# Gated linear attention with stacked gate products, transferred rotation of the queries and halved square sums, in a two-block network on one core

## The reference, cut to what matters

```python
g = log_sigmoid(lowrank @ w_gk + b_gk) / 16        # forward and backward, rank 16 each
q = apply_rope(rms_norm_2(q, q_norm), cos, sin)    # a head's quarters 0,1 and 2,3 change places
p = softmax(q @ k.T * 128 ** -0.5)
o, _ = gla_chunked(q_g, k_g, v_g, g, s0)           # forward and backward, added
y = rms_norm_2(o, g_norm) * silu(gate)             # a head is 256 wide: two tiles of 128
```

## Time and profile before

| what | us |
|---|---|
| median of 3 runs (2815.57 to 2822.95) | 2822.2 |
| the profiled execution, its own time | 2820.59 |
| its span, first to last instruction | 2818.8 |
| PE busy in the span | 2741.7 (97%) |
| DVE busy | 1572.7 (56%) |
| ACT busy | 861.2 (31%) |
| one head, from one `gate_z(·, 0)` to the next (1891.21 to 2004.09) | 112.9 |

### The profile page before, as it was taken

One profiled execution on the slowest core, in us unless ns is written; L12 is line 12 of the kernel. 1 busy time (PEld: TensorE's weight loads), 2 busy tenths in 40 slices (PEclk: granted clock), 3 DMA queues, 4 the chain that ended last, 5 costly groups with the idle time before them and its releaser, 6 DMA issues.

```text
span 2818.8 us, 33294 instructions
## 1 busy us (share of the span) xinstructions
PE 2741.7 (97%) x12970; PEld 2287.3 (81%) x12970; DVE 1572.7 (56%) x2127; ACT 861.2 (31%) x958; POOL 75.7 (3%) x151
## 2 busy tenths in 40 slices
PE   6999999999999999999999999999999999999999
PEld 5888878888888888888788887788888888778887
DVE  5745547636577366645763445667666533564433
ACT  3222234112142121422322323454545522332211
POOL 0000000000000000000000000000000000000000
PEclk9999999999999999999999999999999999999999
DMA  7634523635436355322453422111111342223222
GB/s 279 240 125 171 198 86 117 227 104 203 157 124 230 113 181 183 106 98 96 157 198 101 149 90 96 46 38 57 53 39 43 122 146 96 83 90 103 92 100 79
DMA packets 92935, 353.46 MB, mean 125 GB/s; under 512 B 10528, under 2 KB 11296, under 8 KB 84000
## 3 DMA queue, kind: packets, MB, share of 16 engines
q1 hardware_dynamic: 73120, 250.05, 26.4%
q0 software_dynamic: 19280, 101.23, 9.9%
q10 hardware_dynamic: 432, 0.75, 0.1%
HBM read 343.60 MB, written 8.39 MB: 125 GB/s over the span
## 4 chain that ended last, share of the span: by engine, by line
PE 89%; DVE 6%; ACT 2%; issue 1%; DMA 1%; SPq 0%; DVEq 0%; ACTq 0%
PE ps L1832 23%; PE ps L1834 23%; PE ps L1833 23%; PE ps L2017 4%; PE ps L2019 4%; PE ps L2018 4%; PE ps L2259 1%; DMA w_raw<-in_units 1%; DVE w_raw_lo L1040 1%; PE ps L2207 1%; DVE h_lo L1176 1%; DVE w_lo L1040 0%; PE ps L2112 0%; ACT w_hi L592 0%; PE ps L2253 0%
## 5 line engine op out<-in xcount | busy, mean ns | idle before, releaser
L1832 PE MATMUL ps<-h_hi,w_hi 128*128 128x512 f32 x1936 | 756.5, 391 | 10.8 <-DVE h_lo L1176 4.6
L1833 PE MATMUL ps<-h_lo,w_hi 128*128 128x512 f32 x1936 | 754.7, 390 | 0.0
L1834 PE MATMUL ps<-h_hi,w_lo 128*128 128x512 f32 x1936 | 754.7, 390 | 0.0
L592 ACT CAST w_hi<-w_raw 128x2048 fp32r<-128x2048 f32 (+1 forms) x240 | 422.0, 1758 | 616.4 <-PE ps L1834 520.9
L1040 DVE TENSOR_TENSOR w_lo<-w_raw,w_hi 128x2048 fp32r<-128x2048 f32 (+1 forms) x219 | 458.3, 2093 | 132.5 <-ACT w_hi L592 132.3
L1832 PEld LDWEIGHTS ps<-h_hi,w_hi 128*128 128x128 f32 x1936 | 364.4, 188 | 90.2 <-issue 11.0
L1834 PEld LDWEIGHTS ps<-h_hi,w_lo 128*128 128x128 f32 x1936 | 364.3, 188 | 76.3
L1833 PEld LDWEIGHTS ps<-h_lo,w_hi 128*128 128x128 f32 x1936 | 364.5, 188 | 75.3
L1832 PE MATMUL ps<-g_hi,w_hi 128*128 128x512 f32 x960 | 373.5, 389 | 0.0
L1833 PE MATMUL ps<-g_lo,w_hi 128*128 128x512 f32 x960 | 373.4, 389 | 0.0
L1834 PE MATMUL ps<-g_hi,w_lo 128*128 128x512 f32 x960 | 373.4, 389 | 0.0
(11 more groups left out here) (331 smaller groups left out, 2931.2 us busy)
## 6 DMA issues: line engine op xcount, KB each, us to landing
w_raw<-in_units SPq DMA_DIRECT2D x350, 512.0 KB, 4.5
ada<-in_ada_t POOLq DMA_DIRECT2D x56, 1024.0 KB, 6.9
w_raw<-in_units SPq DMA_DIRECT2D x128, 352.0 KB, 3.7
ada<-in_ada_t POOLq DMA_DIRECT2D x64, 512.0 KB, 5.0
ada_first<-in_ada_t SPq DMA_DIRECT2D x8, 1024.0 KB, 18.1
x_res<-in_x SPq DMA_DIRECT2D x4, 512.0 KB, 8.1
x_home<-x_res POOLq DMA_DIRECT2D x1, 2048.0 KB, 6.5
attn_home<-attn_out POOLq DMA_DIRECT2D x8, 256.0 KB, 2.3
```

The costliest lines, as they stand in the source:

```text
L592: nc.scalar.copy(W_HI[u.slot][:, 0:n], W_RAW[u.slot][:, 0:n]).then_inc(hi_done, 1)
L1832: pe.matmul(dst, hi[:, k, c], rhs_hi(k), start=(k == 0), stop=False)
L1833: pe.matmul(dst, hi[:, k, c], rhs_lo(k), start=False, stop=False)
L1834: last = pe.matmul(dst, lo[:, k, c], rhs_hi(k), start=False, stop=(k == kt - 1))
```

## The change

1. **Stacked gate products.** `U_LR` holds the low-rank weights three times (96 columns, unit of 768 columns instead of 256). ACT rounds its result into `LRT` (96 rows, two copies), and DVE replaces rows 32 to 63 by the rest. The gate's weights come as 96 rows, already block-diagonal, into the scratch `SSQ` by one transfer; ACT rounds them (`gate_weights_hi`), DVE forms the rest in rows 64 to 95 (`gate_weights_lo`). `gate_z` is then one fp32r product over 96 rows (hi·hi + lo·hi + hi·lo). GpSimd's clearing of `W_GK` goes. On SP the first of these loads waits for `ms_made` 7 (end of L2008) and not for `wgk_zero`.
2. **Rotation by transfers.** The two products with PERM go. SP copies `QX` to `TQ` in eight transfers of 32 partitions by 512 (`swap_queries`), behind `q_evac`; `q_turned` waits for `q_swapped` and reads `TQ` instead of the banks. `q_root` waits for the squares alone (`q_ms`).
3. **Squares added on VectorE.** `out_sums` adds the two tiles of squares; `out_squares` on PE has four products instead of eight.
4. **Five-part queries.** `queries` has parts of 1, 2, 1, 2 and 2 blocks k; the first stands ahead of `gate_z(i+1, 0)`, the others around the gate and norm products.
5. **One exp-ln set.** Before the gate's first Exp, ACT loads a set that holds Exp and Ln, so that L814 and the first `decay` Exp behind it need no load.
6. Order: ACT's `split_hi` and DVE's `split_lo` of the next head's value unit (U_G+4i+6) move ahead of `decay_in(·, 0)` and of `q_scale`. Some semaphores are merged (no change of order).

```diff
-    return KD * 2 * RANK if n == U_LR else FULL
+    return KD * GATE_ROWS if n == U_LR else FULL
...
                 if i == 0:
-                    sp.wait_ge(wgk_zero, 1)
+                    sp.wait_ge(ms_made, 7)
...
+                sp.dma_start(W_GK_RAW, ins["w_gk"][:, i, :]).then_inc(wgk_landed, 16)
+
+            def swap_queries(i):
+                sp.wait_ge(q_evac, i + 1)
+                for m in range(2):
+                    for b in range(4):
+                        sp.dma_start(TQ[m][32 * b:32 * b + 32, :], QX[m][32 * (b ^ 1):32 * (b ^ 1) + 32, :]).then_inc(q_swapped, 16)
...
+            def gate_weights_hi(i):
+                act.wait_ge(wgk_landed, 16 * (i + 1))
+                if i > 0:
+                    act.wait_ge(z_made, 2 * i)
+                nc.scalar.copy(W_GK[0:GATE_ROWS].rearrange("p d m -> p (d m)"), W_GK_RAW).then_inc(wgk_hi, 1)
...
             def gate_exp(i, d):
+                if d == 0:
+                    nc.scalar.preload_act_table_set("natural_log_exp_and_others")
...
+            def gate_weights_lo(i):
+                low = slice(4 * RANK, GATE_ROWS)
+                dve.wait_ge(wgk_hi, i + 1)
+                w = W_GK[low].rearrange("p d m -> p (d m)")
+                nc.vector.tensor_tensor(w, SSQ[low, 0:2 * P], w.bitcast(F32), ALU.subtract).then_inc(wgk_made, 1)
...
+            def out_sums(i):
+                dve.wait_ge(o_sq, 2 * i + 2)
+                nc.vector.tensor_tensor(O_SQ[0], O_SQ[0], O_SQ[1], ALU.add).then_inc(o_ssq, 1)
...
             def q_turned(i, m):
+                dve.wait_ge(q_swapped, 128 * (i + 1))
                 nc.vector.tensor_tensor(QX[m][:], QX[m][:], COS[:], ALU.mult)
-                nc.vector.tensor_tensor(TQ[m][:], BANK[4 + m], SIN[:], ALU.mult).then_inc(q_sin, 1)
+                nc.vector.tensor_tensor(TQ[m][:], TQ[m][:], SIN[:], ALU.mult).then_inc(q_sin, 1)
...
-                for m in range(2):
-                    last = pe.matmul(BANK[4 + m], PERM[:], QX[m][:], start=True, stop=True)
-                last.then_inc(q_rot, 1)
...
                 for c in range(NC_):
-                    for e in range(2):
-                        last = pe.matmul(BANK[2][:, c:c + 1], O_SQ[e][:, c * CH:(c + 1) * CH], ONES_D[:, 1:2], start=(e == 0), stop=(e == 1))
+                    last = pe.matmul(BANK[2][:, c:c + 1], O_SQ[0][:, c * CH:(c + 1) * CH], ONES_D[:, 1:2], start=True, stop=True)
...
                 if i + 1 < GH_:
+                    queries(i + 1, 0)
                     gate_z(i + 1, 0)
-                    queries(i + 1, 0)
+                    queries(i + 1, 1)
                     out_squares(i)
+                    queries(i + 1, 2)
                     gate_z(i + 1, 1)
-                    queries(i + 1, 1)
+                    queries(i + 1, 3)
                     out_scales(i)
-                    queries(i + 1, 2)
+                    queries(i + 1, 4)
                     gk_gq(i + 1, 0)
-                    query_turns(i + 1)
+                    query_squares(i + 1)
```

More of the change, by code:

```diff
@@ L406, in build @@
         q_evac = sem("q_evac")
+        o_ssq = sem("o_ssq")
+        q_swapped = sem("q_swapped")
         v_made = sem("v_made")
@@ L484, in _ @@
             ffn(3)
-            unit(at(U_LR), KD * 2 * RANK)
+            unit(at(U_LR), KD * GATE_ROWS)
             sp.wait_ge(evac_done, U_LR)
@@ L927, in rounds @@
                 out_squares(i)
+            low_rank_hi()
+            gate_weights_hi(0)
             split_hi(at(U_K))
@@ L939, in _ @@
             key_root()
-            decay(0, 0)
-            decay(0, 1)
+            decay_out(0, 0)
+            decay_in(0, 0)
+            decay_out(0, 1)
+            decay_in(0, 1)
             kq_out(0)
@@ L1707, in _ @@
                     decay_arg(i + 1, 1)
+                    split_lo(at(U_G + 4 * i + 6))
                     q_scale(i + 1)
@@ L1710, in _ @@
                     q_turned(i + 1, 1)
-                    split_lo(at(U_G + 4 * i + 6))
                     decayed(i + 1, 0)
@@ L2111, in gate_z @@
                 for a, b in ((0, T), (T, TA)):
-                    last = pe.matmul(PS[:, 6 * T + a:6 * T + b], W_GK[0:2 * RANK, d, :], LRT[0:2 * RANK, a:b], start=True, stop=True)
+                    last = pe.matmul(PS[:, 6 * T + a:6 * T + b], W_GK[0:GATE_ROWS, d, :], LRT[0:GATE_ROWS, a:b], start=True, stop=True)
                 last.then_inc(z_made, 1)
@@ L2122, in queries, with query_squares @@
                     pe.wait_ge(lo_done, u.v + 1)
-                last = h_products(u, [BANK[4], BANK[5]], (range(0, 3), range(3, 6), range(6, 8))[part])
-                if part == 2:
+                last = h_products(u, [BANK[4], BANK[5]], (range(0, 1), range(1, 3), range(3, 4), range(4, 6), range(6, 8))[part])
+                if part == 4:
                     last.then_inc(pe_done, 1)
-            def query_turns(i):
+            def query_squares(i):
                 pe.wait_ge(z_out, 2 * i + 2)
@@ L2133, in query_turns @@
                     for c in range(4):
-                        pe.matmul(BANK[6][:, 4 * m + c:4 * m + c + 1], Q_SQ[m][:, c * P:(c + 1) * P], ONES_HD[:, 0:1], start=True, stop=True)
-                pe.wait_ge(q_evac, i + 1)
-                for m in range(2):
-                    last = pe.matmul(BANK[4 + m], PERM[:], QX[m][:], start=True, stop=True)
-                last.then_inc(q_rot, 1)
+                        last = pe.matmul(BANK[6][:, 4 * m + c:4 * m + c + 1], Q_SQ[m][:, c * P:(c + 1) * P], ONES_HD[:, 0:1], start=True, stop=True)
+                last.then_inc(q_ms, 1)
             def own_scores(i):
@@ L2332, in _ @@
             own_scores(0)
-            for part in range(3):
+            for part in range(5):
                 queries(0, part)
-            query_turns(0)
+            query_squares(0)
             for i in range(GH_):
@@ L2464, in feature_tiles, with gate_rows @@
     return np.asarray(rows)[0].T.reshape(KD, P, -1).transpose(1, 0, 2)
+def gate_rows(inputs):
+    w = np.zeros((3, 2 * RANK, GH_, 2, P), np.float32)
+    for d, name in enumerate(("w_gk_fwd_2", "w_gk_bwd_2")):
+        w[:, RANK * d:RANK * (d + 1), :, d, :] = np.asarray(inputs[name])[0].reshape(RANK, GH_, P)
+    return w.reshape(GATE_ROWS, GH_, 2 * P)
 def layouts(inputs):
```

105 lines of the change are left out of this document (59 added, 46 removed).

## The result

The changed kernel takes 2795.08 us (median of 4 runs, 2794.94 to 2795.95), the kernel before beside it 2820.39 us (2815.57 to 2822.95): a ratio of 0.9912, 95% interval 0.9897 to 0.9926. The prediction was 2794.5 us. The profiled execution has a span of 2793.4 us, against 2818.8 before.

What follows compares the result with a forecast made beforehand. TensorE (PE), busy in 97% of the span, was taken as the bound. Terms 24.6 (8.2 x 3) + 3.9 + 0.8 - 0.65 - 1.2 - 1.35 = 26.1 us off 2820.59 gave 2794.5, range 2786 to 2808.

Steps and rivals of the forecast that it cites:

- two gate products: Each change of heads, TensorE: two plain float32 products become one fp32r product each, 1.33 us saved twice, 2.66.
- clock: Each change of heads: the granted clock's drop to 0.50 behind squares and second gate product goes, 1.6 us saved.
- value weights' wait: Each change of heads: TensorE's wait for the value unit's rest goes, as split_lo comes ahead of the rotation, 0.9 us.
- VectorE's margin: Changes of heads: VectorE's 3.68 us in hand before the first row maximum are used up to 0.2 us.
- The transfers: The queries' rotation: eight transfers issued one every 0.475 us, each landing 2.2 us after issue.
- Head 0: Gates save 3.9 us; the rotation loses 0.65 by a later start and 1.2 by half clock after idling.
- Ahead of head 0: U_V's issue waits for ms_made 7, loss 1.0 us; the wider low-rank unit on VectorE, 0.35; 1.35 lost in sum.
- Behind head 3: Behind the last head: ScalarE's 0.78 us wait for the squares goes, 0.8 us saved.
- Transfers landing late: Rival, chance 0.12: the last transfer takes 5.0 us instead of 2.2 to land, 10.5 us lost, so 2805.
- The clock still dropping: Rival, chance 0.10: the clock still drops at each change of heads, 3 x 1.6 us back, 2799.
- The rounds taking part back: Rival, chance 0.06: VectorE enters the rounds without its 3.68 us; with 1.5 us more per head, 2800.
- Not doing what it says, or slower: Slower, chance 0.02: the rotation becomes the bound; 10 us of landing gives 2825. Same has 0.02 too.

Runs made afterwards that it cites:

- e3: The changed kernel with the gate products of the same 96 stacked rows as plain float32 products: 2804.01 us.
- e11: e6 with the gate products over 32 rows of plain float32 values, as in the kernel before, instead of 96: 2812.6 us.
- e5: The changed kernel with the queries in the three parts of before, squares and second gate product side by side: 2797.24 us.
- e4: The changed kernel with the squares of a head's two halves summed on TensorE again, without VectorE's addition: 2797.42 us.
- e1: The changed kernel with the queries' rotation back on TensorE in every head (two PERM products behind the squares), no transfers: 2796.49 us.
- e6: The changed kernel with the edits of e1, e3, e4 and e5 together; table set, split_lo order and gate weights' path stay: 2808.32 us.
- e9: The changed kernel with the value weights' rest (split_lo) behind the rotation on VectorE again: 2818.56 us, ratio to the kernel before 0.9995.
- e8: The changed kernel with each of the eight transfers cut in two, sixteen of 16 partitions, to land about 5 us later: 2815.47 us.
- e7: The changed kernel without the combined table set of exponential and logarithm: 2799.46 us.
- e2: The changed kernel with PERM products on TensorE in head 0 alone and transfers in heads 1 to 3: 2792.21 us.
- e10: The changed kernel with head 0's gate weights issued behind the value unit U_V instead of ahead of it: 2794.44 us.
- c1: The changed kernel with PERM products in head 0 alone, as in e2, and ScalarE's v_out ahead of the fourth level's exponentials: 2784.95 us, ratio to before 0.9878.

## Why the prediction held, term by term

**A change of heads.** Predicted 8.4 on TensorE, 8.2 taken; measured 8.4 (25.3 in three).

| term | predicted | measured | from |
|---|---|---|---|
| two gate products | 2.66 | 2.4 | e3 1.9 + 0.5 of e11 for the 32 rows |
| wait for `at_made`, with the order | 0.5 | 0.7 | e5 |
| squares | 0.85 | 1.0 | e4 |
| permutation | 1.9 | 1.7 | e1 |
| clock | 1.6 | 1.6 | e11, first change against the others |
| value weights' wait | 0.9 | 1.2 | what is left: before 45.2, e11 with its drop 44.0 |
| sum | 8.4 | 8.6 | 45.19 - 36.75 = 8.4 by the marks |

The sizes hold to 0.3 us each. The gate term was a little high: from a gate product's start to the second product behind it the trace before has 1.79 and 1.82 us (the prediction gives 1.69), the trace after 0.59, so two save 2.4 and not 2.66. One reason is not shown: the clock's. That the drop would go was right, and so was its price. But parting the pieces is not needed (no drop in e5 and e6), and two of e11's three changes have the pair in full and no drop. Whether shortening it is what took the drop away stays open; that the term came out as large as predicted is in part luck. The last term is a remainder, not measured by an edit that undoes it alone; e9 does not give it, since with the transfers that order costs 8.1.

**VectorE's margin.** "Used up to 0.2, so every us by which transfers land later is lost in each head": the size holds in e8, 5.0 us in each change and its rounds for 5.2 us of delay. The mechanism is shown by e7 and not by e8: in e7 VectorE's 0.55 us turn up as 0.6 in the rounds at full clock, while in e8 the 1.8 us of the rounds are at the same time TensorE's half clock behind its wait, a term that the prediction had for head 0 alone. The layout put the first row maximum 8.2 us earlier; measured from the last attention product ahead of it, it came 8.1 earlier (1927.14 - 1886.58 = 40.56 against 1936.66 - 1888.01 = 48.65).

**The transfers.** The predicted landing was right (2.2, measured 2.0), the predicted spacing was not: it was taken from the tables' loads, 0.475 us each, and these are issued every 0.63. Timeline of SyncE, after, head 0:

```profile
1806.87 5.03 SPq L508 DMA_DIRECT2D attn_tq<-attn_qx  x8
```

In the changes this took nothing more than the margin, by the first row maximum above. In head 0 it is on the path. The Trainium skill (DMA: Bandwidth & Descriptors, Bandwidth) has 0.95 us for 64 KB, by which the eight would have taken an estimated 7.6 us; the trace has 5.03, so it was on the other side. The halves of e8 are issued one every 0.63 us too, so what the string costs in these two kernels goes by the number of transfers and not by their bytes.

**Head 0.** Here the forecast was most wrong: 3.9 - 0.65 - 1.2 = 2.05 saved, measured 0.2 (136.6 to 136.4; 135.9 to 137.1 in the kernels that leave head 0 alone). The part that saves was about right: with the permutation back (e1) head 0 is 4.1 shorter than before, 0.7 of it by the earlier root told below. The failed term is the transfers' price, 0.65 + 1.2 = 1.85, measured 3.9 against e1 and 4.5 against e2. The half clock is 1.5 of the 3.9, near the 1.2. The rest is 2.4 instead of 0.65: 1.1 by the slower issue (7 x 0.155), and 0.7 because the comparison was made against the old rotation's start, 4.9 us behind the copy's end (1811.57 to 1816.43). ScalarE's root waited for the permutation products then; with `q_ms` signalled ahead of them, as e1 has it, the rotation starts after 4.2 (1808.47 to 1812.63). The parts that save also have runs of their own. e3 makes head 0 2.7 longer, which looks like the predicted 2.66, but only 1.9 of it lie ahead of the first scores; with the 0.5 for 32 rows that is 2.4, as in a change, and the other 0.8 lie in a column that strays by 1.2. e7 makes it 1.5 longer (predicted 1.28). What the table set brings behind the changes, 0.6 in each set of rounds, had no term of its own in the prediction.

**Ahead of head 0.** Predicted 1.35 lost; G alone can't tell it. Counted from block one's last `x_res` operation (1711.19 in the earlier trace rows), SyncE issues `U_V` after 4.0 us before, 3.0 in e10 and 4.5 in eleven of the twelve kernels with the wait (4.9 in e4); the prediction had 6.2 (1717.4). The step that failed is the end of `ms_made` 7. It was taken from the earlier trace rows, where the four column sums of a tile (eight records) take 1.85 us; after, they take 1.03. Timeline of TensorE, after:

```profile
1713.20 1.03 PE L2059 MATMUL ps<-ones_d,g_t 128*128 128x1 f32 x8
```

The granted clock is 0.54 and 0.50 during these sums before (1713 to 1717), 0.60 and 0.50 in e10; in e1 it is 1.00 in 1713 to 1715. Why they ran slowly in just the two kernels in which SyncE doesn't wait for them is open. "Cast about 5.4 later since the tables ahead of it are through by then" failed the other way: from issue to cast it is 6.0 to 8.0 us in the twelve, as it was 6.6 before. The two errors nearly cancel, and a loss of 0 to 0.7 instead of 1.0 is left. VectorE's wider operation was sized about rightly: `x_res` starts 0.66 us behind TensorE's last product ahead of it instead of 0.42, so 0.24 instead of 0.35.

**Behind head 3.** Predicted 0.8 saved; the trace after seems to say 0.9 lost (from the last A to the next unit's first product 29.2 us against 28.3). Timelines behind the last head, first after, then e10:

```profile
2217.68 8.70 SPq L462 DMA_DIRECT2D w_raw<-in_units  x4
...
2230.69 0.77 PE L2068 MATMUL ps<-a_hi,w_hi 128*128 128x512 f32 x1 [5.15 <-issue]
```

```profile
2220.20 8.61 SPq L462 DMA_DIRECT2D w_raw<-in_units  x4
...
2227.12 1.90 ACT L600 CAST w_hi<-w_raw 128x2048 fp32r<-128x2048 f32 x1 [7.56 <-DMA w_raw<-in_units]
...
2231.45 0.47 PE L2068 MATMUL ps<-a_hi,w_hi 128*128 128x512 f32 x1 [3.47 <-issue]
```

In e10, with the same program there, the unit is cast 6.9 us after its issue, in the profiled execution after 8.7 (2226.37 - 2217.68). The load takes 6.8 to 7.1 us from issue to cast in all other kernels but e5 (8.3). From the last A to that product the six kernels with VectorE's addition and an ordinary load and issue take 27.5 to 28.1 us, mean 27.8 (e1, e3, e7, e8, e9, e10), the four with both halves on TensorE 28.2 to 28.4, mean 28.3 (before, e4, e6, e11): 0.5 saved of the predicted 0.8. Why the load was slow in two executions is open, and so is why e2 and c1, the two with the permutation in head 0 alone, issue it 17.7 us behind the last A and the others of that kind after 16.2 to 16.9.

**The rivals.** Transfers landing late: no, 2.0 us. The clock still dropping: no. The rounds taking part back: no, 67.5 in both, though e7 shows that they do as soon as VectorE is any later. Not doing what it says, or slower: no. That the total came out only 0.6 us off is luck: head 0 (1.9 worse) and what lies ahead of it (2.6 better, mostly by scatter) pulled against each other, as did the changes (0.7 better) and the tail (2.1 worse, by scatter).

## What to carry to other kernels

Cut the profiles at marks that all variants share, and learn from untouched stretches how far one profile can be read: here to 0.1 us in one stage and to 2.8 in another. Look at the granted clock of every stretch before a loss is put down to an engine's delay: in e8 both were there at once. When a step moves from the bound engine to one with time in hand, work out what its queue does once that time is used up: with the transfers in place, one instruction of 2.3 us behind them instead of ahead of them costs 23 us (e9), where in the kernel before it cost some 1 us in a change. A thing that pays in a steady stage may cost in the first, where the bound engine is idle; treat the first pass apart, as c1 does.
